# Expert loop of a mixture-of-experts layer: the down products move one block back, the weights come in halves, and ScalarE loads the down weights from its own queue

## What is computed

```
expert_id = g_sel[:, None] * EXPERTS_PER_GROUP + top_i       # two experts for each token, of 32
padded = ((counts + MOE_BLOCK - 1) // MOE_BLOCK) * MOE_BLOCK  # blocks of 128 rows, one expert each
block_e = searchsorted(pend, arange(n_blocks) * MOE_BLOCK)    # expert of each block, ascending
hid = silu(xb @ w_gate[e]) * (xb @ w_up[e])                   # xb: 128 x 1024, hid: 128 x 512
out = hid @ w_down[e]                                         # 128 x 1024
```

## Time and profile before

| | |
|---|---|
| median of 3 runs | 2601.83 us (2600.53 to 2602.84) |
| the profiled execution's own time | 2598.93 us |
| its span, first to last instruction | 2597.2 us |
| TensorE, VectorE, ScalarE busy, share of the span | 84%, 55%, 43% |
| mean granted TensorE clock | 0.923 of full speed |
| first gate product of the expert loop | 1542.63 us |

### The profile page before, as it was taken

One profiled execution on the slowest core, in us unless ns is written; L12 is line 12 of the kernel. 1 busy time (PEld: TensorE's weight loads), 2 busy tenths in 40 slices (PEclk: granted clock), 3 DMA queues, 4 the chain that ended last, 5 costly groups with the idle time before them and its releaser, 6 DMA issues. The chain is left out here.

```text
span 2597.2 us, 29608 instructions
## 1 busy us (share of the span) xinstructions
PE 2193.0 (84%) x9806; PEld 1650.3 (64%) x9807; DVE 1421.5 (55%) x2441; ACT 1110.1 (43%) x1586; POOL 276.6 (11%) x348
## 2 busy tenths in 40 slices
PE   4999999948969687876999549999999999999950
PEld 3764444448447576765888437777777777777740
DVE  4831582045258576674544557566648847354548
ACT  6101111012317576665222126566647847355432
POOL 0002331024220110000000000000000000000022
PEclk6999999979869898998999759999999999999985
DMA  7023443172742514311433158477758958454649
GB/s 223 33 73 138 170 142 118 41 245 112 314 112 69 114 27 88 86 29 51 134 128 134 51 218 347 186 282 279 279 210 340 370 227 333 168 198 195 253 172 378
DMA packets 128019, 458.76 MB, mean 177 GB/s; under 512 B 25136, under 2 KB 41536, under 8 KB 113600
## 3 DMA queue, kind: packets, MB, share of 16 engines
q1 hardware_dynamic: 98352, 345.22, 38.0%
q0 software_dynamic: 18928, 69.49, 7.1%
q10 hardware_dynamic: 10656, 43.00, 4.0%
HBM read 342.06 MB, written 115.61 MB: 176 GB/s over the span
## 5 line engine op out<-in xcount | busy, mean ns | idle before, releaser
L1533 DVE TENSOR_TENSOR w_gate_lo<-w_gate_raw,w_gate_hi 128x2048 fp32r<-128x2048 f32 x64 | 146.3, 2286 | 179.0 <-ACT w_gate_hi L1488 179.0
L895 DVE CUSTOM_DVE_ANT_0 scores<-c_bank,alibi 128x512 f32<-128x512 f32 (+3 forms) x320 | 175.4, 607 | 109.0 <-PE c_bank L993 108.8
L488 PE MATMUL a_bank<-w_in_chunk,hT 128*128 128x512 f32 x512 | 221.9, 596 | 0.7 <-ACT hT L266 0.7
L488 PE MATMUL a_bank<-hT,w_in_chunk 128*128 128x512 f32 x512 | 220.6, 593 | 0.0
L300 ACT ACTIVATE proj_out<-a_bank 128x512 f32<-128x512 f32 x64 | 38.2, 597 | 398.7 <-PE a_bank L488 389.4
L488 PEld LDWEIGHTS a_bank<-w_in_chunk,hT 128*128 128x128 f32 x512 | 128.8, 252 | 92.7 <-issue 62.6
L1007 PE MATMUL c_bank<-v_head,map_T 128*128 128x128 f32 x1088 | 152.2, 289 | 41.7 <-ACT map_T L951 41.7
L1576 PE MATMUL m_bank<-w_gate_hi,rows_T_hi 128*128 128x512 f32 x392 | 154.9, 395 | 24.2 <-DVE rows_T_lo L1537 24.2
L1614 PE MATMUL m_bank<-w_down_hi,hidden_T_hi 128*128 128x512 f32 x392 | 160.4, 409 | 16.2 <-ACT hidden_T_hi L1510 16.2
L488 PEld LDWEIGHTS a_bank<-hT,w_in_chunk 128*128 128x128 f32 x512 | 97.0, 190 | 120.9 <-issue 120.8
L1007 PEld LDWEIGHTS c_bank<-v_head,map_T 128*128 128x128 f32 x1088 | 136.2, 198 | 57.4 <-ACT map_T L951 57.4
(11 more groups left out here) (375 smaller groups left out, 4427.0 us busy)
## 6 DMA issues: line engine op xcount, KB each, us to landing
w_gate_raw<-in_w_gate_dram SPq DMA_DIRECT2D x32, 2048.0 KB, 7.8
w_up_raw<-in_w_up_dram SPq DMA_DIRECT2D x32, 2048.0 KB, 10.7
w_down_raw<-in_w_down_dram SPq DMA_DIRECT2D x32, 2048.0 KB, 10.7
rows_d<-rows_out ACTq DMA_DIRECT2D x50, 512.0 KB, 10.3
rows_d<-zero_rows POOLq DMA_DIRECT2D x34, 512.0 KB, 18.6
x_tile<-in_x_dram SPq DMA_DIRECT2D x16, 512.0 KB, 3.8
w_in_chunk<-in_w_in_dram POOLq DMA_DIRECT2D x4, 2048.0 KB, 14.9
qT_d<-xn_tile SPq DMA_DIRECT2D x32, 256.0 KB, 3.1
```

What stands on the lines that cost most here:

```text
L488: last = pe.matmul(bank[4 + n % PB][:], lhsT, rhs, start=kt == 0, stop=kt == KT - 1)
L895: dve.tensor_tensor_reduce(S[:, s, m, c * BANK:c * BANK + w], bank[n % 4][:, 0:w], bias[:, h % 2, x0:x0 + w], 1.0, -BIG, ALU.add, ALU.max, ...
L1533: dve.tensor_tensor(wlo[w][:, s], raw[w][:, s], whi[w][:, s], ALU.subtract).then_inc(lo_done[w], 1)
```

## The change

Five things are done.

1. On TensorE a pass now makes the gate product of block j+1, turns `hidden` of block j, makes the up product of block j+1, turns the eight parts of the rows of block j+2, and makes the down product of block j. The first block's gate and up products stand ahead of the loop, the last block's down product behind it. No wait for `hidden` or `hidden_T_hi` follows at once on the work that makes them.
2. Each weight has a semaphore and a DMA for each half, and a half is loaded as soon as its own lo part is made.
3. The loads of the down weights are issued by ScalarE, at the end of a pass, after a wait for the lo part of each half (`lo_done[2]`), which VectorE makes at the end of its pass. SyncE issues gate and up.
4. In a pass with a new expert VectorE splits both gate halves ahead of `hidden` and of `rows_T_lo`. ScalarE copies both halves of the output. In the loop ScalarE reads four values of the table in each pass, the last of them (the next expert's number) at a place that depends on the second.
5. The table of ScalarE's functions is loaded once ahead of the loop.

Lines below are those of the changed kernel, cut to the loops.

```
             @block.scalar
...
+                with act.Fori(0, later(act)) as j:
+                    before, now, order = place(act, j), place(act, j + 1), place(act, j + 2)
+                    e = expert(act, now + 1)
+                    hidden_hi(j + 1)
+                    act.wait_ge(g_done, j + 2)
+                    act.wait_ge(hid_done, j + 1)
                     act.activation(sil[:], G[:], ACT.Silu).then_inc(silu_done, 1)
                     with where_below(nc, act, now, order):
+                        split_hi(0, order, 0)
+                        split_hi(0, order, 1)
+                    rows_hi(0, 2 * j + 5)
+                    rows_hi(1, 2 * j + 6)
                     with where_below(nc, act, now, order):
+                        act.wait_ge(u_done, j + 2)
+                        split_hi(1, order, 0)
+                    out_half(0, j)
                     with where_below(nc, act, now, order):
+                        split_hi(1, order, 1)
+                    out_half(1, j)
+                    store(j)
+                    with where_below(nc, act, before, now):
+                        split_hi(2, now, 0)
+                        split_hi(2, now, 1)
+                        for i in range(2):
+                            act.wait_ge(lo_done[2], 2 * now + 3 + i)
+                            load(act, 2, e, i)
...
             @block.vector
...
+                with dve.Fori(0, later(dve)) as j:
+                    before, now, order = place(dve, j), place(dve, j + 1), place(dve, j + 2)
+                    hidden_lo(j + 2)
                     with where_below(nc, dve, now, order):
+                        split_lo(0, order, 0)
+                        split_lo(0, order, 1)
+                    hidden(j + 1)
+                    rows_lo(0, 2 * j + 5)
+                    rows_lo(1, 2 * j + 6)
                     with where_below(nc, dve, now, order):
+                        split_lo(1, order, 0)
+                        split_lo(1, order, 1)
+                    with where_below(nc, dve, before, now):
+                        split_lo(2, now, 0)
+                        split_lo(2, now, 1)
...
             @block.tensor
...
+                with pe.Fori(0, later(pe)) as j:
+                    before, order = place(pe, j), place(pe, j + 1)
+                    pe.wait_ge(xh_done, 2 * j + 4)
+                    pe.wait_ge(xl_done, 2 * j + 4)
...
+                    product(G, 0, g_done)
+                    hidden_T(j)
...
+                    product(U, 1, u_done)
+                    pe.wait_ge(x_in, 16 * j + 48)
+                    rows_T(0)
+                    rows_T(1)
+                    down(j, before)
+                end = later(pe)
+                hidden_T(end)
+                down(end, place(pe, end))
```

More of the change, by code:

```diff
@@ L1483, in _, with split_hi @@
             @block.scalar
             def _(act):
[L1485 to L1488, removed]
+                def split_hi(w, order, i):
+                    act.wait_ge(w_in[w][i], 16 * order + 16)
+                    act.activation(whi[w][:, halves[i]], raw[w][:, halves[i]], ACT.Copy).then_inc(hi_done[w], 1)
@@ L1496, in _, with store @@
+                def store(b):
+                    act.wait_ge(d_used, 2 * b + 4)
+                    act.dma_start(d["rows"][bass.ds(b, 1)].rearrange("o p n -> p (o n)"), out[:]).then_inc(out_st, 16)
+                e = expert(act, 0)
+                for i in range(2):
+                    load(act, 2, e, i)
+                act.preload_act_table(ACT.Silu)
                 rows_hi(0, 1)
                 rows_hi(1, 2)
[L1498 to L1501, removed]
-                        split_hi(0, order, (0,))
-                    act.wait_ge(g_done, b + 1)
-                    act.wait_ge(hid_done, b + 1)
+                for w in range(3):
+                    split_hi(w, 0, 0)
+                    split_hi(w, 0, 1)
@@ new lines, in _ @@
+                first, second, e = place(act, 0), place(act, 1), expert(act, 1)
+                act.wait_ge(g_done, 1)
+                act.activation(sil[:], G[:], ACT.Silu).then_inc(silu_done, 1)
+                with where_below(nc, act, first, second):
+                    split_hi(0, second, 0)
+                    split_hi(0, second, 1)
+                for i in range(2):
+                    act.wait_ge(lo_done[2], 3 + i)
+                    load(act, 2, e, i)
+                rows_hi(0, 3)
@@ L1525, in _ @@
+                out_half(1, end)
+                store(end)
+                for i in range(2):
+                    act.wait_ge(w_in[2][i], 16 * final + 32)
+                act.wait_ge(out_st, 16 * end + 32)
                 act.activation(last_copy[:], ones[:, 0:1], ACT.Copy)
@@ new lines, in _ @@
+                for w in range(3):
+                    split_lo(w, 0, 0)
+                    split_lo(w, 0, 1)
+                first, second = place(dve, 0), place(dve, 1)
+                with where_below(nc, dve, first, second):
+                    split_lo(0, second, 0)
+                    split_lo(0, second, 1)
+                hidden(0)
+                rows_lo(0, 3)
+                rows_lo(1, 4)
+                with where_below(nc, dve, first, second):
+                    split_lo(1, second, 0)
+                    split_lo(1, second, 1)
```

173 lines of the change are left out of this document (87 added, 86 removed).

## The result

The changed kernel takes 2630.44 us (median of 4 runs, 2627.89 to 2633.42), the kernel before 2602.18 (4 runs): the ratio is 1.011, with an interval from 1.0092 to 1.0127. It is slower by 28 us. The forecast was 2647 with a range from 2612 to 2668.

The account below looks back on a forecast made before the run. TensorE was taken as the bound. 1548.6 + 24 x 18.2 + 19 x 21.3 + 5 x 21.9 + 28 + 2 + 17 = 2546.6, against 2501.9 before, +45: median 2647 us, range 2612 to 2668.

Parts of the forecast that it names:

- Direction and cause: ScalarE's wait for VectorE's second down lo half holds up its next pass; 0.84 chance of slower, 2647 us forecast.
- the one table load ahead of the loop: ScalarE's function table loads, 1.28 us each, lie beside TensorE's work, so removing them wins nothing by itself.
- The passes: Pass j is late if blocks j-1 and j+1 are both followed by a new expert: 24 of 48, five long.
- A pass on time: TensorE pass in which nobody is late: 16.8 of matmuls plus 1.4 of turns, 18.2 us.
- The second register read on TensorE costs nothing: TensorE's added table read is free, since its one read before left no gap behind the down matmuls.
- The chain of a late pass: ScalarE's wait, issue and reads put `hidden_T_hi` at 12.0; next gate product at 21.3 us, 21.9 in runs of changes.
- the reads: Four table reads on ScalarE behind the load's issue, 0.72 each with register work; with the loop's turn 3.2 us.
- The clock: TensorE at 1.2 GHz after idling about 3 us: 1.4 us for each of 19 stretches and the start, 28 us.
- Rival A: Late passes happen but TensorE's clock stays up: 28 us less, 2619; chance 0.18.
- Passed by nothing: SyncE's queue: gate and up only lose the down load between them; costed at nothing.
- the loads on ScalarE win nothing: Queues share the same 16 engines, so ScalarE's loads save at most 0.34 us of SyncE's time, which nobody waits for.
- Start, down, end: Second gate product at about 1548.6; six passes with `hidden_T_hi` late for down, 2 us; last pass 17 in all.

Follow-up runs that it names:

- the first experiment: Changed kernel with the down loads on SyncE, behind gate and up; ScalarE neither waits nor issues and reads three values: 2617.86 us.
- in order: Changed kernel with SyncE issuing all loads, an expert's down behind the next expert's gate and up; ScalarE neither waits nor issues: 2531.18 us.
- rows first: Changed kernel with the rows (and on VectorE hidden) split ahead of both gate halves on ScalarE and VectorE: 2600.14 us.
- kept busy: Changed kernel with twenty extra turns of `ident` on TensorE at the end of passes whose next product needs a new gate: 2660.57 us.
- in order with the wait: The 2531.18 us version with ScalarE again waiting for both lo halves of down and reading one value behind, no load issued: 2597.97 us.
- wait alone: Changed kernel with SyncE issuing down behind gate and up; ScalarE keeps both waits and the fourth read, issues nothing: 2660.43 us.
- six reads: Changed kernel with two more table reads, six instead of four, at the top of ScalarE's pass: 2655.08 us.

## Why the prediction was right, step by step

**Direction and cause.** Slower, because of ScalarE's blocking wait: shown. With the wait and the issue taken off ScalarE, and its loads moved to SyncE in the order in which tiles come free, the kernel is 99 us faster (2531.18); with the wait and a read alone put back, 67 of them are gone. Of the rest of the change that version lacks only one of ScalarE's four reads and a load of down weights at the end that nothing used. That the one table load ahead of the loop wins nothing was not tried by itself.

**The passes.** All 24 passes named, and no other, are late, and the five long ones are those named (pass 1, at 21.1, lies between). That step rested on the times of the gate loads alone.

**A pass on time.** 18.2 was forecast, 18.16 to 18.24 measured. "The second register read on TensorE costs nothing" held.

**The chain of a late pass.** `hidden_T_hi` at 12.0 was forecast, 11.38 measured. The second lo half was ready at 8.0 (8.1 forecast), the issue ended at 8.5 (8.7). The term that was mis-sized is the reads. I took 0.72 for a read with its register work, out of a median of 0.50 and a stretch of 2.07 us. In the changed kernel they stand 0.62 apart:

```profile
L1454 ACTq TENSOR_LOAD <-block_meta x147: 272/282/1282, 1528.2 to 2521.6; - x147
```

This is the line that reads the table, on ScalarE's queue (ns, min, median, max). The read itself now takes the 0.28 that was its least before. Up to the end of the issue the chain was 0.2 shorter than forecast, the turn and the reads 0.4 shorter, the work behind 0.2 longer: 20.87 instead of 21.3, and 21.3 in runs instead of 21.9. The floor of about 600 ns that the Trainium skill puts under a tensor_load ("DMA: Bandwidth & Descriptors", Latency and other measured facts) is not seen for the read alone; it is close to the distance from one read to the next, 0.62.

**The clock.** Forecast 20 stretches of 1.4 us, 28 in all. Measured: 18 that count (17 passes of 19.78 and the last), at 1.6 us, 29. Rival A, 0.18, is out: in passes 1 to 47 19 of 22 waits of 2.5 us or more were followed by a lower clock (two of them in late passes, where it cost nothing).

**SyncE's queue.** "Passed by nothing" was right for the change, and the reason that I gave for why the loads on ScalarE win nothing was incomplete. The Trainium skill's Key Constraints ("Trainium Kernel Development and Optimization") let them win the issue time only. No run contradicts that for the transfers: all six of a pass from one queue came in time. But a queue is also an order. In the first experiment, with SyncE's old order, the gate loads stand behind down's wait, and that costs 87 us against the same loads in order (2617.86 against 2531.18). A second queue avoids it too. The prediction had no price for it, because it never asked what SyncE's queue would look like with the split of down moved by a block. The change pays with a wait on an engine that is needed; SyncE in the right order does it for nothing.

**Start, down, end.** The second gate product was forecast for 1548.6 and came at 1543.53. SyncE's first gate load was issued at 1508.87 and not at 1513.53, so 4.7 of the 5.1 us are in the stages ahead, which is chance and not foresight (last section). Six passes late for down, 2 us: none, pass 16 took 18.16. The last block: 18.5 rather than 17, since its down product, behind a wait of 10.2 us, ran its first matmuls 0.43 apart and took 7.6 us where 5.7 was forecast.

**The sum.** Against 2546.6: start -5.1, late passes 19 x -0.43 and 5 x -0.57 = -11.0, passes on time -0.7, clock +1, down -2, end +1.5: -16.3. The loop ended at 2530.74, 15.9 earlier than forecast, and this is the whole gap between 45 us and the 29.0 by which the two spans, 2626.2 and 2597.2, differ.

## What to carry to other kernels

A semaphore wait blocks everything behind it on its engine, DMA issues, register reads and the next pass among them, so put a load that has to wait for a tile on a queue whose engine has nothing else to do, and order that queue by when the tiles come free. When a step is moved by a block, move its load in the queue with it. Price idle time of TensorE with the slower clock that may follow it, which here added 1.6 us to most waits of 2.5 us.

## What the runs showed of the hardware

**The clock depends on the length of the wait, and not surely.** Waits of TensorE ahead of a gate product, from the second block's on (its wait stands by itself), and how many were followed by a stretch at 1.2 GHz:

| wait (us) | lower clock | kernels |
|---|---|---|
| 0.7 to 1.76 | 0 of 54 | rows first 30, kept busy 20, changed 2, in order with the wait 2 |
| 1.8 to 1.94 | 13 of 36 | in order with the wait 7 of 19, wait alone 5 of 15, kept busy 1 of 2 |
| 2.05 to 2.46 | 7 of 14 | in order with the wait 3 of 3, kept busy 4 of 8, six reads 0 of 3 |
| 2.5 to 2.8 | 34 of 43 | changed 19 of 22, six reads 15 of 21 |
| over 5 | 18 of 18 | down loads on SyncE, wait alone |
| second block, 2.58 to 2.68 | 7 of 9 | all nine |

What decides between equal waits, I can't tell from these runs. In the changed kernel a pass with such a stretch took 19.78 instead of 18.16 to 18.24.

**Reads of a register value from the table** took 0.28 us on ScalarE in the changed kernel and 0.50 in the median before. Before, the first of the two in a pass took 0.29 in the median and the second 0.54; what slowed the second wasn't tried.

**TensorE's sequencer can be the bound.** With twenty short turns at the end of a pass, the turn of the loop and three reads left TensorE idle for 1.0 us behind late passes and for 1.9 to 2.25 behind passes on time. With matmuls of the down product there instead, two or three reads left no gap.

**The stages ahead of the loop vary by 20 us.** SyncE's first gate load was issued at 1500.41 (in order), 1508.87 (changed), 1513.53 (before) and 1519.97 (down loads on SyncE), though between the first and the last of these no edit touches the stages ahead (the changed kernel adds one value to the table that `route` writes):

```profile
1519.97 0.90 SPq L1464 DMA_DIRECT2D w_gate_raw<-in_w_gate_dram  x2
```

So the start of a stage has to be taken off before two profiled loops are compared, and single runs of the kernel before lay between 2585 and 2611 us.
